# Attention output in a hybrid decoder layer: the probabilities become the weights, V with one column of ones is streamed, and the result is transposed by the crossbar

## The chip, the cores and the metric

The kernel runs on the 8 cores of one Trainium2 chip. Each core takes two of the sixteen sequences (4096 tokens) and all the weights, and exchanges nothing with the other cores. The time is device microseconds of the slowest core for one call. Matrix products run on TensorE (PE; PEld is its loading of weights), the rest on VectorE (DVE), ScalarE (ACT) and GpSimd (POOL); most transfers are issued from SyncE (SP).

## The reference, cut to what matters

One layer: a gated feed-forward half step, a mixing part, and a second gated feed-forward half step, all with RMS norms before them and residuals around them. The mixing part has causal latent attention (8 heads, 96 wide queries and keys, 64 wide values), a short gated convolution, sigmoid gates over both, and an output projection. The change touches only this:

```python
def one_block(args):
    qb, blk = args
    scores = jnp.einsum('bqhd,bkhd->bhqk', qb, k).astype(jnp.float32) * scale
    ...
    p = jax.nn.softmax(scores, axis=-1).astype(v.dtype)
    return jnp.einsum('bhqk,bkhd->bqhd', p, v)
...
y_a = causal_block_attention(q, k, v) @ w_proj_attn
```

x is (16, 2048, 1024) float32; D_FF is 2816. All products run in bf16 with float32 sums.

## The kernel before

**Order of the work.** Nobody writes the order of the instructions by hand. The program records operations with `op(eng, fns, cost, reads, writes)` and DMAs with `dma(...)`, each with a cost in microseconds, a key (how early it is wanted) and the tiles that it reads and writes. `Sched.order` then plays the program through four times with these costs, five queues (PE, ACT, DVE, POOL, SP), the PSUM banks and one DMA pipe, turns the place of each PE operation into due times for what feeds it (`deadlines`), and keeps the order with the shortest played length. `emit` writes each queue in that order with the semaphore waits that are needed. A queue runs strictly in its order: an instruction that waits holds up all behind it, on SP too. So an edit to one operation's cost or tiles can move instructions of every engine.

**Stages.** FFN1 over four blocks of 1024 tokens (L1061 gate and up, L1088 down), the mixing part over eight groups of 512 tokens (four per sequence), FFN2. In the mixing part the functions `qkv`, `attn`, `conv`, `merge` and `outp` of a group are recorded one after the other, and the scheduler interleaves groups: matmuls of the convolution and the merge fill PE while ACT makes the probabilities.

**Attention** (`attn`, L1260). For group g the query block is qb = g mod 4, and its key tiles are kt = 0 to 4 qb + 3, so 4, 8, 12 or 16 tiles of 128 keys. For each of 8 heads and each key tile:

- PE multiplies the 128 keys (weights) with the queries streamed, which gives scores with keys on partitions and up to 512 queries in the free dimension (L1273). On the four diagonal tiles only 512, 384, 256 and 128 queries are left.
- ACT takes the exponential into one of four bf16 tiles `pt` (L1277). On a diagonal tile POOL multiplies the first 128 columns by a triangle (L1280).
- PE multiplies `Vc` (weights) with `pt` streamed (L1282) and sums over the key tiles in one PSUM bank O. `Vc` holds, for each pair of heads, 64 columns of V, 64 of ones, and 64 of V of the other head. A 128 column window of it gives 64 partitions of output and 64 partitions that all hold the sum of the probabilities.

After a head's last key tile DVE makes four instructions (L1288, L1289, L1291, L1293): a transpose of the sums in 32 by 32 blocks from PSUM, a reciprocal of 16 columns, a transpose back, and the product of O with it, written to `atT` in bf16. `atT` has the attention output with channels on partitions, which is what the projection `ya` in `merge` streams (L1306, the rows `pb<-atT,rng`).

There are 640 (group, head, key tile) steps on a core: 448 with 512 queries, of which 384 are off the diagonal, and 64 each with 384, 256 and 128. O may take one of the banks 0 to 5, the scores too.

**Weights of the mixing part** come through a ring of eight tiles `rng` in pieces of eight matmuls (256 KB in bf16, four matmuls for `ya`), loaded by SP (`wpiece`, `dmm`, L1296 to L1306). The projections out of the latents are transposed by DMA_TRANSPOSE from SP, SBUF to SBUF (`ltT`, `KT`, `QT`). The V part of it is copied from PSUM to `Vc` by ACT (L1230), and its ones are written once by POOL (L1141).

**Memory** is laid out by hand: tiles of FFN2 share addresses with tiles of the mixing part, and the scheduler turns each overlap into a dependence. `U` (L684) is the address at which the tiles of the second half begin.

## Time and profile before

| | |
|---|---|
| three timed runs | 3454.61, 3130.39, 3073.76 us; median 3130.39 |
| the profiled execution | 3071.06 us |
| its span on the slowest core (core 7) | 3069.5 us |
| spans of the eight cores | 3061.7 to 3069.5 us |
| mean granted TensorE clock of each core | 0.998 to 1.000 |
| mixing part, about | 953 to 2119 us of the span |

The rows below are of core 7. Times in them are microseconds from the start of the span; a matmul's duration includes the time until its last result is written, so durations of consecutive matmuls overlap, and the time that one takes of PE is read from the distance of the starts. A row with "x8" merges eight consecutive instructions, and its length runs from the first start to the last end. Of the three timed runs the profiled execution is next to the fastest.

### The profile page before, as it was taken

How to read it: one execution, taken by the hardware profiler on the slowest of the kernel's cores; microseconds unless marked ns; L12 is line 12 of the kernel's file. 1: busy time of each engine (PE TensorE's matmuls, PEld its weight loads, DVE VectorE, ACT ScalarE, POOL GpSimd, SP SyncE). 2: the span in 40 equal slices, each digit the busy share in tenths (PEclk: the TensorE clock that was granted, in tenths of full speed). 3: DMA queues.
4: the chain of work that ended last, by engine and by line, in shares of the span. 5: the costliest groups of instructions: out<-in, count | busy, mean ns of one | idle time of the engine just before them, and what ended most of it. 6: DMA issues, size and time to landing. Idle time of an engine off the chain costs nothing.

```text
span 3069.5 us, 44192 instructions; the slowest of 8 cores (3061.7 to 3069.5 us)
## 1 busy us (share of the span) xinstructions
PE 3038.8 (99%) x14464; PEld 1408.0 (46%) x14464; DVE 1096.8 (36%) x1605; ACT 1008.2 (33%) x1798; POOL 754.3 (25%) x1415
## 2 busy tenths in 40 slices
PE   7999999999999999999999999999999999999999
PEld 3444444444444444444444444444444444444444
DVE  4232132133245564544755646443311121111111
ACT  2122112112124556668536475772210110110110
POOL 2111011111054544443645535321110000000000
PEclk9999999999999999999999999999999999999999
DMA  8967757997645676655785858567784564232212
GB/s 179 164 160 175 185 182 153 168 220 171 126 100 137 156 184 153 161 150 117 193 201 153 198 139 193 139 161 201 153 145 123 125 184 131 76 100 100 76 56 89
DMA packets 347980, 458.55 MB, mean 149 GB/s; under 512 B 200688, under 2 KB 210160, under 8 KB 346352
## 3 DMA queue, kind: packets, MB, share of 16 engines
q1 hardware_dynamic: 309744, 311.74, 38.9%
q0 software_dynamic: 31680, 120.93, 21.6%
q10 hardware_dynamic: 6336, 23.07, 1.9%
q8 instruction: 123, 2.02, 0.3%
q14 instruction: 97, 0.79, 0.1%
HBM read 394.63 MB, written 107.81 MB: 164 GB/s over the span
## 4 chain that ended last, share of the span: by engine, by line
PE 96%; DMA 1%; DVE 1%; issue 1%; POOL 0%; SPq 0%; ACT 0%; DVEq 0%; POOLq 0%; ACTq 0%
PE pb L1061 39%; PE pb L1306 22%; PE pb L1088 20%; PE pb L1282 4%; PE pb L1273 4%; PE pb L1375 4%; PE pb L1168 2%; PE pb L1207 1%; PE pb L1211 1%; DMA rng<-w 1%; DMA xr<-x 0%; DMA xin<-x 0%; ACT pt L1277 0%; SPq L1371 0%; DVE zb L1330 0%
## 5 line engine op out<-in xcount | busy, mean ns | idle before, releaser
L1061 PE MATMUL pb<-hT,gu 128*128 128x512 bf16 x5632 | 1220.2, 380 | 1.6 <-DVE hT L1010 1.6
L1061 PEld LDWEIGHTS pb<-hT,gu 128*128 128x128 bf16 x5632 | 551.5, 98 | 667.3 <-issue 5.2
L1088 PE MATMUL pb<-wd,actT 128*128 128x512 bf16 x2816 | 609.9, 379 | 0.0
L1065 ACT ACTIVATE sg<-pb 128x512 f32<-128x512 f32 x352 | 210.1, 597 | 1211.6 <-PE pb L1061 1211.6
L1306 PE MATMUL pb<-hM,rng 128*128 128x512 bf16 x2560 | 583.3, 379 | 0.9 <-ACT pt L1277 0.8
L1067 DVE TENSOR_TENSOR actT<-sg,pb 128x512 bf16<-128x512 f32 x352 | 241.9, 687 | 929.2 <-PE pb L1061 927.8
L1277 ACT ACTIVATE pt<-pb,negM,rK 128x512 bf16<-128x512 f32 (+3 forms) x640 | 409.9, 714 | 76.1 <-PE pb L1273 73.6
L1088 PEld LDWEIGHTS pb<-wd,actT 128*128 128x128 bf16 x2816 | 275.5, 98 | 331.7
L1306 PEld LDWEIGHTS pb<-hM,rng 128*128 128x128 bf16 x2560 | 249.3, 98 | 293.1 <-issue 3.0
L1092 DVE SCALAR_TENSOR_TENSOR xr<-pb,xr 128x512 f32<-128x512 f32 x128 | 88.3, 691 | 369.5 <-PE pb L1088 365.0
L1048 POOL DMA_DIRECT2D gu<-w x88 | 47.2, 536 | 663.1 <-PE pb L1061 575.4
L1350 DVE SCALAR_TENSOR_TENSOR tg<-tg,pb 128x512 f32<-128x512 f32 x128 | 87.9, 687 | 300.7 <-PE pb L1306 208.5
L895 POOL DMA_DIRECT2D gu<-ws x88 | 49.0, 557 | 549.3 <-DMA w<-gu 279.2
L1282 PE MATMUL pb<-pt,Vc 128*128 128x512 bf16 (+3 forms) x640 | 175.4, 348 | 3.2 <-POOL pt L1280 2.0
L1273 PE MATMUL pb<-QT,KT 96*128 96x512 bf16 (+3 forms) x640 | 173.0, 348 | 2.2 <-DVE atT L1293 1.2
L1280 POOL TENSOR_TENSOR pt<-pt,trib 128x128 bf16<-128x128 bf16 x256 | 108.9, 434 | 243.6 <-ACT pt L1277 238.4
L1353 POOL TENSOR_TENSOR mg<-tg,tg 128x512 bf16<-128x512 f32 x64 | 81.0, 1265 | 217.0 <-DVE tg L1350 216.5
L1347 ACT ACTIVATE tg<-pb,hb 128x512 f32<-128x512 f32 x128 | 88.2, 689 | 127.6 <-PE pb L1306 118.7
L1306 PE MATMUL pb<-cvT,rng 128*128 128x512 bf16 x512 | 120.8, 379 | 1.0 <-DVE cvT L1333 0.6
L1375 PE MATMUL pb<-rng,mg 128*128 128x512 bf16 x512 | 118.7, 379 | 0.7 <-ACT pt L1277 0.4
L1330 DVE SCALAR_TENSOR_TENSOR zb<-ub,par_sb,zb 128x512 f32<-128x512 f32 x128 | 102.8, 803 | 24.9 <-ACT zb L1328 20.8
L918 ACT ACTIVATE ho<-xr 128x1024 bf16<-128x1024 f32 x32 | 33.8, 1058 | 212.5 <-DVE xr L1092 203.4
(113 smaller groups left out, 1959.0 us busy)
## 6 DMA issues: line engine op xcount, KB each, us to landing
rng<-w SPq DMA_DIRECT2D x448, 256.0 KB, 3.7
gu<-ws POOLq DMA_DIRECT2D x88, 512.0 KB, 7.8
gu<-w POOLq DMA_DIRECT2D x88, 512.0 KB, 4.5
xr<-x SPq DMA_DIRECT2D x67, 512.0 KB, 5.0
w<-gu ACTq DMA_DIRECT2D x44, 512.0 KB, 4.9
w<-ws POOLq DMA_DIRECT2D x32, 522.0 KB, 21.6
x<-xr SPq DMA_DIRECT2D x32, 512.0 KB, 4.5
xm<-x SPq DMA_DIRECT2D x64, 256.0 KB, 6.1
```

Source lines behind the costliest of these rows:

```text
L1061: op("pe", [lambda e, k=k, a=a, b=b, i=i, sl=sl: e.matmul(bank(b), lhsT=gu[i][:, a, k, :], rhs=hT[sl][:, k, :], start=(k == 0), stop=(k == ...
L1065: op("act", lambda e, q=q, bg=bg: e.activation(out=sg[q][:], in_=bank(bg), func=AF.Silu), c_act(512), bg.deps, [d_sg[q]])
L1067: m = op("dve", lambda e, q=q, bu=bu, c=c, j=j: e.tensor_tensor(out=actT[:, j, c, :], in0=sg[q][:], in1=bank(bu), op=ALU.mult), c_dve(512) ...
L1088: op("pe", [lambda e, k=k, b=b, hf=hf, j=j, u=u: e.matmul(bank(b), lhsT=actT[:, j, k, u * 128:(u + 1) * 128], rhs=wd[:, k, hf * 512:(hf + ...
L1092: op("dve", lambda e, i=i, b=b, hf=hf: e.scalar_tensor_tensor(out=xr[i][:, hf * 512:(hf + 1) * 512], in0=bank(b), scalar=0.5, in1=xr[i][:, ...
L1273: op("pe", lambda e, h=h, kt=kt, j0=j0, n=n, s_=s_: e.matmul(bank(s_)[:, 0:n].rearrange("p (a b) -> p a b", b=128), lhsT=KT[kt // 4][0:96, ...
L1277: op("act", lambda e, i=i, s_=s_, n=n, kt=kt, h=h: e.activation(out=pt[i][:, 0:n], in_=bank(s_)[:, 0:n], func=AF.Exp, scale=rK[g // GPS][: ...
L1280: op("pool", lambda e, i=i: e.tensor_tensor(out=pt[i][:, 0:128], in0=pt[i][:, 0:128], in1=trib[:], op=ALU.mult), c_pool(128), [d_pt[i][0], ...
L1282: op("pe", lambda e, i=i, h=h, kt=kt, c0=c0, n=n, lo=lo, O=O: e.matmul(O()[:, c0:512], lhsT=Vc[kt // 4][:, kt % 4, h // 2, :, :].rearrange ...
L1306: op("pe", [lambda e, k=k: e.matmul(bank(b), lhsT=wv[:, k, :], rhs=rhs(k), start=(k == 0), stop=(k == K - 1)) for k in range(K)], c_mm(*[5 ...
L1330: op("dve", lambda e, q=q, k_=k_, w0=w0: e.scalar_tensor_tensor(out=zb[q][:], in0=ub[q][:, k_:k_ + 512], scalar=par[:, w0 + k_:w0 + k_ + 1 ...
L1375: op("pe", [lambda e, k=k, tt=tt, b=b, W=W: e.matmul(bank(b), lhsT=mg[:, k, tt * 128:(tt + 1) * 128], rhs=W[k // 2][0][:, (k % 2) * 512:(k ...
```

## The change

Operands of the second product are exchanged. For each 128 queries of a `pt` tile one matmul has these 128 columns of `pt` as weights and `Vc` of one head streamed, now 64 columns of V and a single one: 65 columns. Its output has queries on partitions: 64 channels and the sum, at columns 65j to 65j+64 of the same PSUM bank. The four query tiles of a step off the diagonal are one operation of four matmuls. On a diagonal tile the first query tile, which POOL masks, is an operation of its own, behind that of the others, so that the others don't wait for POOL. Query tile j is no longer multiplied with key tiles beyond its diagonal, as before.

A head then needs two DVE instructions: the reciprocal of four columns and the product of 4 times 64 columns with it, into the new tile `aq` (queries on partitions, bf16, one buffer for all groups). After the eighth head SP issues four DMA_TRANSPOSE, each of 128 queries by 512 channels, from `aq` to `atT`. `Vc` shrinks from 6 KB to 4.0625 KB a partition and sequence quarter, and about it all addresses move (`U` from 103.625 to 99.75); `r16` goes and `rec` becomes small.

```diff
-    r16, mk = sb("r16", [128, 16], F32)
-    d_r16 = [mk("0"), mk("1")]
+    rec, mk = sb("rec", [128, 2, 4], F32)
+    d_rec = [mk(f"{i}", 16 * i, 16 * i + 16) for i in range(2)]
...
-    U = 103.625
+    U = 99.75
...
-        t, mk = sb(f"Vc{i}", [128, TPG, 4, 3, 64], BF16)
+        t, mk = sb(f"Vc{i}", [128, TPG, NH, 65], BF16)
...
-        d_at.append([[mk(f"{c}{h}", c * 1024, c * 1024 + 1024) for h in range(2)] for c in range(4)])
+        d_at.append([mk(f"_{tt}") for tt in range(TPG)])
...
+    aq, mk = sb("aq", [128, TPG, 512], BF16)
+    d_aq = [[mk(f"{tt}{h}", tt * 1024 + h * 128, tt * 1024 + h * 128 + 128) for h in range(NH)] for tt in range(TPG)]
...
-        op("pool", lambda e, q=q: e.memset(Vc[q][:, :, :, 1, :], 1.0), 1.3, writes=d_V[4 * q:4 * q + 4], key=LB + 220 if q == 0 else MB - 250)
+        op("pool", lambda e, q=q: e.memset(Vc[q][:, :, :, 64:65], 1.0), 1.3, writes=d_V[4 * q:4 * q + 4], key=LB + 220 if q == 0 else MB - 250)
...
-            op("act", lambda e, st=st, v_=v_, p=p: e.activation(out=Vc[st // 4][:, st % 4, :, 0:3:2, :], in_=bank(v_).rearrange("p (a b d) -> p a b d", a=4, b=2),
+            op("act", lambda e, st=st, v_=v_, p=p: e.activation(out=Vc[st // 4][:, st % 4, :, 0:64], in_=bank(v_).rearrange("p (h d) -> p h d", h=8),
...
-                op("pe", lambda e, i=i, h=h, kt=kt, c0=c0, n=n, lo=lo, O=O: e.matmul(
-                    O()[:, c0:512], lhsT=Vc[kt // 4][:, kt % 4, h // 2, :, :].rearrange("p a d -> p (a d)")[:, lo:lo + 128], rhs=pt[i][:, 0:n],
-                    start=(kt == 0), stop=(kt == nkt - 1), skip_group_check=True),
-                   c_mm(n), [d_V[kt], d_pt[i]], [dO])
-            dn, p_ = 64 - lo, slice(lo, lo + 64)
-            dr, d16 = d_rec[h % 2], d_r16[h % 2]
-            op("dve", lambda e, p_=p_, dn=dn, O=O: e.transpose(out=rec[p_, :], in_=O()[dn:dn + 64, :]), 0.71, [dO], [dr])
-            op("dve", lambda e, p_=p_: e.reciprocal(out=r16[p_, :], in_=rec[p_, :].rearrange("p (b i) -> p b i", i=32)[:, :, 0]),
-               0.26, [dr], [d16])
-            op("dve", lambda e, p_=p_: e.transpose(out=rec[p_, :].rearrange("p (b i) -> p b i", i=32),
-                                                   in_=r16[p_, :, None].broadcast_to([64, 16, 32])), 0.71, [d16], [dr])
-            op("dve", lambda e, p_=p_, h=h, O=O: e.tensor_tensor(out=atT[ql][p_, h // 2, :], in0=O()[p_, :], in1=rec[p_, :],
-                                                                 op=ALU.mult), c_dve(512), [dO, dr], [d_at[ql][h // 2][h % 2]])
+                tiles = [j for j in range(j0, 4) if kt < 4 * qb or j > j0]
+                for first_, js in ((True, tiles), (not tiles, [j0] if kt >= 4 * qb else [])):
+                    if not js:
+                        continue
+                    op("pe", [lambda e, i=i, h=h, kt=kt, j=j, j0=j0, O=O, st_=(kt == 0 and first_ and j == js[0]): e.matmul(
+                        O()[:, j, 0:65], lhsT=pt[i][:, (j - j0) * 128:(j - j0 + 1) * 128], rhs=Vc[kt // 4][:, kt % 4, h, :],
+                        start=st_, stop=(kt == 4 * qb + j), skip_group_check=True) for j in js],
+                       0.031 * len(js), [d_V[kt], d_pt[i][0] if js == [j0] and kt >= 4 * qb else d_pt[i] if kt < 4 * qb else d_pt[i][1]], [dO])
+            dr = d_rec[h % 2]
+            op("dve", lambda e, h=h, O=O: e.reciprocal(out=rec[:, h % 2, :], in_=O()[:, :, 64]), 0.2, [dO], [dr])
+            op("dve", lambda e, h=h, O=O: e.tensor_tensor(out=aq[:, :, h * 64:h * 64 + 64], in0=O()[:, :, 0:64],
+                                                          in1=rec[:, h % 2, :, None].broadcast_to([128, 4, 64]), op=ALU.mult),
+               c_dve(256), [dO, dr], [d_aq[tt][h] for tt in range(TPG)])
+        for tt in range(TPG):
+            sc.key = MB + g * 100 - 87
+            dma("sp", f"aT{ql}{tt}", lambda e, tt=tt: e.dma_start_transpose(
+                out=atT[ql][:, :, tt * 128:(tt + 1) * 128], in_=aq[:, tt, :]), 200000, tr=True, reads=d_aq[tt], writes=[d_at[ql][tt]])
```

**Where instructions move.** First PE at the end of the last group's attention. In the kernel before, L1273 is the score product, L1282 the product with `pt` streamed, L1306 a piece of the convolution or of the merge (the numbers behind a name are those of its buffer and tile):

```order
L1306 MATMUL pb3<-hM1_115,rng6_155 128x512 x8
L1282 MATMUL pb1<-pt2_139,Vc2_132 128x512
L1282 MATMUL pb1<-pt3_140,Vc2_132 128x512
L1273 MATMUL pb0<-QT1_126,KT3_133 128x256
L1273 MATMUL pb1<-QT1_126,KT3_133 128x128
L1306 MATMUL pb3<-hM1_115,rng7_156 128x512 x8
L1282 MATMUL pb1<-pt0_137,Vc3_134 128x512
L1282 MATMUL pb1<-pt1_138,Vc3_134 128x384
L1306 MATMUL pb2<-hM1_115,rng0_149 128x512 x8
L1282 MATMUL pb1<-pt2_139,Vc3_134 128x256
L1282 MATMUL pb1<-pt3_140,Vc3_134 128x128
```

The same stretch of PE in the changed kernel, where the score product is L1272, the changed product L1285 and a piece L1309:

```order
L1285 MATMUL pb1<-Vc2_131,pt3_139 128x65 x4
L1272 MATMUL pb2<-QT1_125,KT3_132 128x256
L1309 MATMUL pb3<-hM1_115,rng7_155 128x512 x8
L1285 MATMUL pb1<-Vc3_133,pt0_136 128x65 x4
L1285 MATMUL pb1<-Vc3_133,pt1_137 128x65 x2
L1272 MATMUL pb1<-QT1_125,KT3_132 128x128
L1309 MATMUL pb3<-hM1_115,rng0_148 128x512 x8
L1285 MATMUL pb1<-Vc3_133,pt1_137 128x65
L1285 MATMUL pb1<-Vc3_133,pt2_138 128x65 x2
L1309 MATMUL pb0<-hM1_115,rng1_149 128x512 x8
L1285 MATMUL pb1<-Vc3_133,pt3_139 128x65
```

Each streamed 512 column product became four of 65 columns, and on the diagonal the masked query tile comes last. Behind this point the kernel before has seventeen pieces of eight matmuls ahead of the first `ya` (the row with `atT`); in the changed kernel the stretch of PE from the last of the attention to `ya` is short enough to show the last part of it whole:

```order
L1309 MATMUL pb3<-hM1_115,rng6_154 128x512 x8
L1309 MATMUL pb0<-hM1_115,rng7_155 128x512 x8
L1309 MATMUL pb1<-hM1_115,rng0_148 128x512 x8
L1309 MATMUL pb2<-hM1_115,rng2_150 128x512 x8
L1309 MATMUL pb2<-cvT_156,rng1_149 128x512 x8
L1309 MATMUL pb0<-atT1_141,rng3_151 128x512 x4
```

Four more such pieces stand ahead of these, so nine are left between the last product with `pt` and the first `ya`. In the other groups more PE work stands between the two, in both kernels.

On SP the four transposes of the last group stand among the loads of the ring in the changed kernel:

```order
L905 DMA rng0_148<-w2 128x1024
L905 DMA rng1_149<-w2 128x1024
L1296 DMA_TRANSPOSE atT1_141<-aq_167 128x4x128
L905 DMA rng2_150<-w2 128x1024
L1296 DMA_TRANSPOSE atT1_141<-aq_167 128x4x128 x3
L905 DMA rng3_151<-w2 128x512
L905 DMA rng4_152<-w2 128x1024
```

The loads of `rng2` and all behind it now stand behind a transpose that waits for the eighth head's DVE instruction; before, nothing of the attention's output stood on SP.

## Rows read from the trace of the kernel before

**Rows 1.** The page's first lines: span, busy time of each engine.

```profile
span 3069.5 us, 44192 instructions; the slowest of 8 cores (3061.7 to 3069.5 us)
PE 3038.8 (99%) x14464; PEld 1408.0 (46%) x14464; DVE 1096.8 (36%) x1605; ACT 1008.2 (33%) x1798; POOL 754.3 (25%) x1415
```

**Rows 2.** The chain of work that ended last, shares of the span by line.

```profile
PE pb L1061 39%; PE pb L1306 22%; PE pb L1088 20%; PE pb L1282 4%; PE pb L1273 4%; PE pb L1375 4%; PE pb L1168 2%; PE pb L1207 1%; PE pb L1211 1%; DMA rng<-w 1%; DMA xr<-x 0%; DMA xin<-x 0%; ACT pt L1277 0%; SPq L1371 0%; DVE zb L1330 0%
```

**Rows 3.** Stretches of the mixing part, 952 to 1100 and 1900 to 2062 us.

```profile
core 7: us, PE busy (x) PEld busy (x) DVE busy (x) ACT busy (x) POOL busy (x), PEclk, DMA share, GB/s
952.00:1100.00 148.00, 142.96 (x712) 68.41 (x711) 90.28 (x141) 91.65 (x165) 83.80 (x157) 0.98 0.58 134
1900.00:2062.00 162.00, 162.00 (x781) 75.31 (x779) 73.68 (x109) 116.69 (x191) 58.27 (x104) 1.00 0.63 164
```

**Rows 4.** Groups by line and shape: busy us, mean ns of one, idle before.

```profile
L1282 PE MATMUL pb<-pt,Vc 128*128 128x512 bf16 x448 | 143.6, 380 | 2.2 <-POOL pt L1280 1.0 <-ACT pt L1277 0.7 <-DVE atT L1293 0.5
...
L1282 PEld LDWEIGHTS pb<-pt,Vc 128*128 128x128 bf16 x640 | 62.1, 98 | 73.2 <-issue 7.5
...
L1282 PE MATMUL pb<-pt,Vc 128*128 128x384 bf16 x64 | 21.2, 331 | 1.0 <-POOL pt L1280 0.9
...
L1282 PE MATMUL pb<-pt,Vc 128*128 128x256 bf16 x64 | 17.6, 275 | 0.0
...
L1282 PE MATMUL pb<-pt,Vc 128*128 128x128 bf16 x64 | 14.1, 220 | 0.0
```

**Rows 5.** Timeline of PE: start us, length us, merged instructions.

```profile
26.63 0.61 PE L1008 MATMUL pb<-idb,xn 128*128 128x128 bf16 x8 [1.51 <-DVE xn L1004]
...
959.91 1.46 PE L1168 MATMUL pb<-wl,hM 128*128 128x384 bf16 x8
...
2061.76 29.52 PE L1306 MATMUL pb<-hM,rng 128*128 128x512 bf16 x136
```

**Rows 6.** Timeline of the weight loads (PEld), same columns.

```profile
962.13 0.10 PEld L1282 LDWEIGHTS pb<-pt,Vc 128*128 128x128 bf16 x1 [0.99 <-issue]
962.16 0.26 PEld L1273 LDWEIGHTS pb<-QT,KT 96*128 96x128 bf16 x2
...
1440.67 0.10 PEld L1273 LDWEIGHTS pb<-QT,KT 96*128 96x128 bf16 x1 [0.43 <-issue]
1440.71 0.10 PEld L1282 LDWEIGHTS pb<-pt,Vc 128*128 128x128 bf16 x1
...
1441.35 0.10 PEld L1273 LDWEIGHTS pb<-QT,KT 96*128 96x128 bf16 x1 [0.54 <-issue]
1441.38 0.10 PEld L1282 LDWEIGHTS pb<-pt,Vc 128*128 128x128 bf16 x1
```

**Rows 7.** Groups of DVE by line and shape.

```profile
L1288 DVE STREAM_TRANSPOSE rec<-pb 64x512 f32<-64x512 f32 x64 | 45.7, 714 | 52.2 <-PE pb L1282 51.1
L1291 DVE STREAM_TRANSPOSE rec<-r 64x512 f32<-64x512 f32 x64 | 45.1, 705 | 5.5
L1293 DVE TENSOR_TENSOR atT<-pb,rec 64x512 bf16<-64x512 f32 x64 | 44.0, 688 | 5.1 <-DVE rec L1291 0.5
...
L1289 DVE RECIPROCAL r<-rec 64x16 f32<-64x16 f32 x64 | 15.8, 248 | 6.0 <-DVE rec L1288 0.5
...
L1176 DVE TENSOR_TENSOR krb<-pb,par_sb 128x32 f32<-128x32 f32 x32 | 5.9, 186 | 7.1 <-PE pb L1168 6.8
```

**Rows 8.** The transposes of `ltT`: ns min/median/max on SP; then us to landing.

```profile
L1174 SPq DMA_TRANSPOSE ltT<-latn x32: 1183/1186/2188, 863.4 to 1907.5; - x32
...
ltT<-latn SPq DMA_TRANSPOSE x32, 3.2
```

**Rows 9.** What PE waited for, and for how long: us, times, longest.

```profile
PE pb L1306 <- DMA rng<-w: 3.5, 2, 3.1
```

**Rows 10.** Timeline of PE after the last group's attention.

```profile
2061.59 0.33 PE L1282 MATMUL pb<-pt,Vc 128*128 128x256 bf16 x2
...
2092.84 1.03 PE L1306 MATMUL pb<-atT,rng 128*128 128x512 bf16 x4
```

More of the change, by code:

```diff
@@ L707, in build_program @@
     d_gain1 = mk()
-    FF.append(ffn_tiles(2, 0, (28, 44.5, U + 50), 36, U, 52.5, U + 58))
+    FF.append(ffn_tiles(2, 0, (28, 42.5, U + 44.25), 36, U, 50.5, U + 52.25))
     at(0)
@@ L745, in build_program @@
     for i in range(2):
-        at((22, U + 50)[i])
+        at((22, U + 44.25)[i])
         t, mk = sb(f"hM{i}", [128, 8, G], BF16)
@@ L759, in build_program @@
     d_rpb = mk()
-    rec, mk = sb("rec", [128, G], F32)
-    d_rec = [mk("0"), mk("1")]
     ltT, d_ltT = [], []
@@ L773, in build_program @@
         if i:
-            at(U + 42)
+            at(U + 36.25)
         t, mk = sb(f"QT{i}", [128, TPG, NH, 128], BF16)
@@ L779, in build_program @@
     for i in range(GPS):
-        at(52.5 if i == 0 else U + 8 * (i - 1))
+        at(50.5 if i == 0 else U + 8 * (i - 1))
         t, mk = sb(f"KT{i}", [128, TPG, NH, 128], BF16)
@@ L783, in build_program @@
         d_KT += [mk(f"{q}", q * 2048, q * 2048 + 2048) for q in range(TPG)]
-        at(60.5 if i == 0 else U + 24 + 6 * (i - 1))
-        t, mk = sb(f"Vc{i}", [128, TPG, 4, 3, 64], BF16)
+        at(58.5 if i == 0 else U + 24 + 4.0625 * (i - 1))
+        t, mk = sb(f"Vc{i}", [128, TPG, NH, 65], BF16)
         Vc.append(t)
-        d_V += [mk(f"{q}", q * 1536, q * 1536 + 1536) for q in range(TPG)]
-    at(66.5)
+        d_V += [mk(f"{q}", q * 1040, q * 1040 + 1040) for q in range(TPG)]
+    at(62.5625)
     rK, d_rK = [], []
@@ L809, in build_program @@
         if i:
-            at(U + 66)
+            at(U + 60.25)
         t, mk = sb(f"atT{i}", [128, 4, G], BF16)
         atT.append(t)
-        d_at.append([[mk(f"{c}{h}", c * 1024, c * 1024 + 1024) for h in range(2)] for c in range(4)])
-    at(75.5)
+        d_at.append([mk(f"_{tt}") for tt in range(TPG)])
+    at(71.5625)
     ub, d_ub, zb, d_zb = [], [], [], []
@@ L828, in build_program @@
     assert place["o"] <= R0 + U * 1024
-    at(U + 58)
+    at(U + 52.25)
     cvT, mk = sb("cvT", [128, 8, G], BF16)
     d_cv = [mk(f"{c}", c * 1024, c * 1024 + 1024) for c in range(8)]
-    at(U + 70)
+    at(U + 64.25)
     mg, mk = sb("mg", [128, 8, G], BF16)
@@ L1264, in attn @@
             sc.key = MB + g * 100 - 95 + h
-            lo = 0 if h % 2 == 0 else 64
             ob = sc.slot(OB)
-            O, dO = lambda ob=ob: bank(ob), ob.deps
+            O, dO = lambda ob=ob: bank(ob).rearrange("p (j d) -> p j d", j=4), ob.deps
             for kt in range(nkt):
```

## The prediction

> **What bounds the kernel now.** I read the page's busy times first: PE is busy 3038.8 of 3069.5 us, no other engine over 36% [rows 1]. Then the chain that ended last: nearly all of it is PE, and the product that is changed (L1282) has 4% of the span [rows 2]. A share over the whole span can hide a stage with another limit, so the third view is the table of stretches of the mixing part [rows 3]. At its end PE is busy 162 of 162 us, with ACT at 117 and DVE at 74. At its beginning it is not quite so: PE 143 of 148, and the granted clock is 0.98, which with the two levels of 2.4 and 1.2 GHz is some 6 us at the lower one. So the kernel is bound by PE, and the change is worth what it takes off or puts on PE's own column of work; everything else counts only if it makes PE wait. The idle time that the mixing part offers is small: 5 us in the first stretch.
>
> Because PE's durations overlap, a matmul's price is the distance between starts. From merged rows it is (length minus the duration of one) over (count minus one) [rows 5, 4]: 512 columns (29.52 - 0.38)/135 = 0.216 us; 384 columns (1.46 - 0.33)/7 = 0.161; 128 columns (0.61 - 0.22)/7 = 0.056, each with a load of other weights between. These lie on one line of 0.000416 us a column, which gives 0.109 for 256.
>
> **PE: what goes.** L1282 has 448 matmuls of 512 columns and 64 each of 384, 256 and 128 [rows 4]: 448 x 0.216 + 64 x (0.161 + 0.109 + 0.056) = 96.8 + 20.9 = 117.6 us. The 4% of the chain (some 123 us) agrees.
>
> **PE: what comes.** 384 steps off the diagonal with four matmuls each, and 64 each with 4, 3, 2 and 1: 1536 + 640 = 2176 matmuls of 65 columns, each with its own load of 128 columns of `pt`. Nothing in the trace has 65 columns. Two things can set the distance:
>
> - The columns. The line above at 65 is 0.056 - 63 x 0.000416 = 0.030 us. A matmul of 65 columns cannot be cheaper than this by the rows, so it is the lower end: 2176 x 0.030 = 65 us, 52 less than before.
> - The load. A load's duration is 98 ns [rows 4], but loads overlap as matmuls do. After a stop of PE two loads of different tiles follow each other at 0.03, 0.04 and 0.03 us, with the first one's matmul issued in between [rows 6]. So a load, the start of its matmul and the next load fit in 0.033 us (the mean of the three, which are rounded to 0.01).
> - The upper end is the row of 128 columns: eight pairs of load and matmul at 0.056 us [rows 5]. A pair with fewer columns and the same load should not cost more: 2176 x 0.056 = 122 us, 4 more than before.
>
> I take the load's distance, 0.033, because it is the later of the two limits and is measured on the loads of this very product: 2176 x 0.033 = 71.8 us. The change on PE is 71.8 - 117.6 = -46 us, with ends at -52 and +4.
>
> The row of 128 columns bears on a rule. The Trainium skill, page "TensorE: Matmul & The Clock Gate", section "Back-to-back issue gap", says that in a stream of load and matmul pairs 128 columns cost about 81 ns each and 512 about 131. The trace has 56 and 216 for these, so it does not bear the rule out; by it 2176 pairs would be 176 us, 59 more than before.
>
> **Other engines.** DVE loses 0.714 + 0.248 + 0.705 + 0.688 = 2.36 us a head and gains a reciprocal of 4 columns and a product of 256. Between the rows of 32 columns (186 ns) and 512 (688 ns) [rows 7] the product is 0.42, and the reciprocal is no more than the 0.25 of 16 columns, say 0.2: 0.62 us. For 64 heads DVE goes from 151 to 40 us. It is off the path; the value on PE lies between 0 and the 5 us of idle and the 3 us of lower clock of the first stretch, where DVE is busy 90 of 148 us [rows 3]. I take 0, since ACT (92) and POOL (84) feed the same chain there. The memset of ones shrinks and the copy of V keeps its 512 columns: both are off the path, and I cost them at nothing under PE's own work.
>
> SP gains 32 transposes of 128 by 512. The nearest row is `ltT` with 128 by 640: 1.19 us on SP and 3.2 us to landing [rows 8]. That is 38 us of SP spread over 1100 us. Their path after the last head of a group is one product on DVE and its wait (0.7), four issues (4.8), one landing (3.2): 8.7 us, where before it was 2.4. `ya` waits for it. The shortest cover is in the last group: before, 31 us lay between the two [rows 10]; now nine pieces of eight matmuls are left, 72 x 0.216 = 15.6 us, so 7 us remain. Behind the first transpose on SP stand ring loads; when it waits for head 8, they wait. The ring holds eight pieces, 8 x 8 x 0.216 = 13.8 us of PE, against some 5 us of issues and the wait before. And the first head of the next group may not write `aq` before all four have landed; DVE would wait, and behind it the convolution's products. Each is covered by the rows, but a miss of some 3 us in a group, as the single wait for `rng` of 3.1 us shows now [rows 9], is possible. I put 0 in the sum, and 3 x 8 = 25 us at the far end.
>
> With PE 46 us faster over the mixing part, the last stretch would have ACT at 117 of some 150 us, still not a bound.
>
> **Sum.** The profiled execution took 3071.1 us (span 3069.5 and 1.6 around it): 3071.1 - 46 = 3025 us. The median of the three timed runs is 3130, 59 us above the profiled one; I forecast against the latter, which agrees with the fastest run within 3 us. 3025 is 1.5% less. About 2% (61 us) is what a measurement of this kernel can tell from no change.
>
> **Rivals.**
>
> 1. *The pair costs what 128 columns cost.* If a load cannot start until the array has taken the whole of the weights before it in, the distance of 0.03 after a stop is a burst and not a rate. Loads stood 0.056 apart in the long row of eight, but there the 128 columns alone explain that. Then 0.056 x 2176 = 122 and the time is 3071 + 4 = 3075. Anything between, say 0.045, gives 3051.
> 2. *PE gets faster, but waits give it back.* Place: merge of each group, by `atT` or by ring loads behind a waiting transpose on SP. Price up to 25 us, time 3025 + 10 to 25, 3035 to 3050. For it: the four queues are in fixed order, and SP is now on the attention's path. Against it: the covers above, 15.6 us against 8.7 at the tightest.
> 3. *More than the columns.* DVE's relief and the masked tile taken last remove the 5 us idle and the lower clock at the start of the mixing part, and the pair runs at the columns' 0.030: 3071 - 52 - 8 - 3 (the wait for `rng`) = 3008, just past 2% less.
> 4. *Slower: load and matmul take turns when the matmul is shorter than the load.* In all rows that I have, the matmul (216 to 380 ns from start to end, 56 or more between starts) covers the load's 98 ns. At 65 columns the load could stand in the open with its full 98 ns [rows 4]: 2176 x 0.098 = 213 us, 96 more than before, time 3167. It decides from 0.082 us a pair on (179 us for all), where the kernel is 2% slower. Against it: the loads 0.03 apart. By the rule of the Trainium skill above the time would be 3130, nearly this case; it shares this rival's chance.
>
> **How the numbers follow.** The forecast with its neighbourhood of 3010 to 3045 has 0.68; rival 1 and what lies between 0.13; rival 2 0.08; rival 3 beyond 2% 0.07; rival 4 0.04. The time is that of the likeliest, 3025. The range reaches from 3003, between rival 3 and the lower end of the pair's price, to 3078, which takes in rivals 1 and 2. Faster by over 2% (under 3010): 0.08. Slower by over 2% (over 3132): 0.04. Within 2%: 0.88.
>
> **What would show it.** The changed product's matmuls should stand 0.033 us apart in rows of four (a merged row of x4 about 0.1 us plus the duration of one), with loads at the same distance; 0.056 or 0.098 would be rivals 1 and 4. PE should still be busy 98 to 99% with a busy time some 46 us lower, DVE's some 111 us lower. In the waits of PE there should be no group `atT` or `rng` over 5 us; if there is, rival 2 holds. [...] The prediction is wrong if the span moves by less than 25 us, or if it moves by 46 for a reason that is not the distance of these matmuls.

## The result, and the profile of the changed kernel

The changed kernel takes 3028.5 to 3034.5 us, against 3073.0 to 3077.6 us of the kernel before; here and below, runs in which one die ran markedly slower at a lower clock are left out on both sides. The ratio is 0.9854, with a 95% interval of 0.9837 to 0.9871: 1.5% faster, some 45 us. The profiled execution of the changed kernel is the slowest of its four, 3034.5 us, and 37 us under the profiled one of the kernel before. The forecast was 3025 us and 46 us of gain.

The page's first lines, which answer to [rows 1] and [rows 2]:

```profile
span 3032.9 us, 47191 instructions; the slowest of 8 cores (3017.7 to 3032.9 us)
## 1 busy us (share of the span) xinstructions
PE 2990.5 (99%) x16000; PEld 1416.4 (47%) x16000; DVE 982.2 (32%) x1477; ACT 1004.2 (33%) x1798; POOL 748.2 (25%) x1415
...
PE pb L1061 40%; PE pb L1309 21%; PE pb L1088 20%; PE pb L1272 4%; PE pb L1378 4%; PE pb L1168 2%; PE pb L1285 2%; DMA rng<-w 1%; PE pb L1207 1%; PE pb L1211 1%; ACT pt L1276 0%; DMA xin<-x 0%; SPq L1296 0%; DVE zb L1333 0%; DMA h<-hq 0%
```

The profiled core is core 4 here, where it was core 7 before. PE has 1536 matmuls more and is busy for 48 us less; the changed product went from 4% to 2% of the chain (L1282 before, L1285 now). DVE lost 115 us. What PE is bound by has not changed.

The groups by line and shape answer to [rows 4] and [rows 7]:

```profile
L1285 PEld LDWEIGHTS pb<-Vc,pt 128*128 128x128 bf16 x2176 | 115.7, 98 | 80.6 <-issue 5.0
L1285 PE MATMUL pb<-Vc,pt 128*128 128x65 bf16 x2176 | 133.9, 194 | 2.0 <-POOL pt L1279 1.0 <-ACT pt L1276 0.6
...
L1291 DVE TENSOR_TENSOR aq<-pb,rec 128x256 bf16<-128x256 f32 x64 | 27.1, 424 | 6.0 <-DVE rec L1290 0.9
L1290 DVE RECIPROCAL rec<-pb 128x4 f32<-128x4 f32 x64 | 11.5, 180 | 66.6 <-PE pb L1285 65.6 <-PE pb L1272 0.8
```

A load still takes 98 ns and a matmul of 65 columns 194 ns from its start to its last result. What they take of PE is again read from the starts. The timeline of PE in the dense part of the last group (start us, length us, merged instructions), and the loads of the same stretch:

```profile
1975.59 0.41 PE L1285 MATMUL pb<-Vc,pt 128*128 128x65 bf16 x8
1976.06 0.29 PE L1285 MATMUL pb<-Vc,pt 128*128 128x65 bf16 x4
1977.48 0.41 PE L1285 MATMUL pb<-Vc,pt 128*128 128x65 bf16 x8
1979.40 0.41 PE L1285 MATMUL pb<-Vc,pt 128*128 128x65 bf16 x8
```

```profile
1975.38 0.50 PEld L1285 LDWEIGHTS pb<-Vc,pt 128*128 128x128 bf16 x8
1975.84 0.38 PEld L1285 LDWEIGHTS pb<-Vc,pt 128*128 128x128 bf16 x4
```

Eight matmuls in 0.41 us are (0.41 - 0.194)/7 = 0.031 us apart, four in 0.29 are 0.032, and four in 0.28, as in rows further down, 0.029. The expectations below use 0.029 or 0.030 for the same distance. With 0.031 the product costs 2176 x 0.031 = 67.5 us, 50 less than the 117.6 before. The row of eight loads is longer only because the first was pulled 0.2 us ahead, into the 512 column matmul before.

So 50 us went off PE's column and 45 off the time. What is between them is net waiting. Idle time of PE in the mixing part of core 7, kernel before and then changed (columns as in [rows 3]):

```profile
952.00:2100.00 1148.00, 1139.68 (x5623) 543.27 (x5622) 631.24 (x965) 695.16 (x1251) 536.11 (x980) 1.00 0.67 164
```

```profile
952.00:2100.00 1148.00, 1131.94 (x7360) 571.21 (x7358) 525.71 (x852) 703.47 (x1266) 541.20 (x989) 1.00 0.73 175
```

PE idles 8.3 us before and 16.1 after (on core 5, 10.8 and 20.3). The cores differ, though all run the same instructions: on the six whose records are complete it is 8.3 to 10.8 us before and 13.7 to 24.3 after. A difference of a few us on one core is therefore no finding by itself. Core 4, the slowest, has the most of these six. This is what happens on it at about 1038 us, PE's timeline and then the stretch:

```profile
1038.24 3.45 PE L1309 MATMUL pb<-cvT,rng 128*128 128x512 bf16 x8 [2.78 <-DMA rng<-w]
```

```profile
1036.00:1042.00 6.00, 3.76 (x10) 1.44 (x11) 0.13 (x1) 0.24 (x1) 0.00 (x0) 0.72 1.14 226
```

PE waits 2.8 us for a ring load, and the eight matmuls behind it span 3.45 us, where eight of this shape span 1.89 us otherwise. The granted clock of the stretch is 0.72, so part of it is at the lower level of 1.2 GHz. The same comes again about a wait of 3.6 us that ends at 1572.4. The mean clock of core 4 is 0.998, which is some 6 us of 3033. Core 7 has the first wait too (2.45 us), but no fall of the clock behind it, and not the second; its mean clock is 1.000, after 0.998 before, and its span fell by 48.7 us.

In the middle of the mixing part the waits are of another kind. On core 4 a stretch of 31 us in the later part of the fourth group's attention has 3.8 us of idle time, with ACT busy for 26.7 of 31:

```profile
1390.00:1421.00 31.00, 27.24 (x237) 14.79 (x234) 8.57 (x17) 26.74 (x50) 9.81 (x23) 1.00 0.61 132
```

The timeline of PE in it:

```profile
1408.91 0.38 PE L1272 MATMUL pb<-QT,KT 96*128 96x512 bf16 x1
1409.13 0.28 PE L1285 MATMUL pb<-Vc,pt 128*128 128x65 bf16 x4
1409.58 0.38 PE L1272 MATMUL pb<-QT,KT 96*128 96x512 bf16 x1 [0.17 <-ACT pt L1276]
1409.80 0.28 PE L1285 MATMUL pb<-Vc,pt 128*128 128x65 bf16 x4
1410.25 0.38 PE L1272 MATMUL pb<-QT,KT 96*128 96x512 bf16 x1 [0.17 <-ACT pt L1276]
1410.47 0.28 PE L1285 MATMUL pb<-Vc,pt 128*128 128x65 bf16 x4
```

Score product and changed product follow each other with no other work between. A step is 0.67 us here, the pace of one exponential on ACT, of which PE needs 0.22 + 0.12. Before, PE needed 0.43 of it. The profile shows only 0.17 us of the 0.33 that are lost in a step as idle: the rest is hidden under the durations of the matmuls, which overlap. So the idle times in this document are lower bounds of the waits.

What PE waited for, on core 4, against the single row [rows 9]:

```profile
PE pb L1309 <- DMA rng<-w: 9.6, 4, 3.6
PE pb L1309 <- DVE cvT L1336: 2.2, 2, 1.6
...
PE pb L1272 <- ACT pt L1276: 1.5, 7, 0.3
```

The waits for ring loads are longest on this core. On the eight cores they are 1.0 to 9.6 us, three of them over the 5 us of the forecast's sign for rival 2 (9.6, 7.4 and 5.1 us on cores 4, 5 and 6); before, they were at most 3.9 us. The transposes, against [rows 8] (their issues by tile, with shortest, median and longest ns; then the row of DMA issues, with the median us to the landing), and the way to `ya` in the last group (PE's timeline on core 7), against [rows 10]:

```profile
L1296 SPq DMA_TRANSPOSE atT<-aq x32: 1188/1194/2292, 986.4 to 2050.9; - x32
```

```profile
atT<-aq SPq DMA_TRANSPOSE x32, 4.4
```

```profile
2033.18 0.19 PE L1285 MATMUL pb<-Vc,pt 128*128 128x65 bf16 x1
2033.21 13.98 PE L1309 MATMUL pb<-hM,rng 128*128 128x512 bf16 x64
2047.03 1.89 PE L1309 MATMUL pb<-cvT,rng 128*128 128x512 bf16 x8
2048.76 1.03 PE L1309 MATMUL pb<-atT,rng 128*128 128x512 bf16 x4
```

`ya` starts 15.6 us after the last product and waits for nothing on this core. On core 4 it waits 1.55 us, not for `atT` but for its ring load, which SP had issued at 2052.3 us, behind the last three transposes (2048.2 to 2052.2). This is rival 2's mechanism, at 1.55 us; in the kernel before a later piece of `ya` waited 3.1 us for its load on core 7, with no transpose of `aq` on SP.

### The profile page after: what moved, and what is told of

Its sections match the earlier page's. It is cut to its first block, busy times and chain, and to the rows that moved or that the text cites. A ratio compares the mean times of both kernels' runs of the same rounds, so it can differ in the third digit from the quotient of the medians.

```text
span 3032.9 us, 47191 instructions; the slowest of 8 cores (3017.7 to 3032.9 us)
## 1 busy us (share of the span) xinstructions
PE 2990.5 (99%) x16000; PEld 1416.4 (47%) x16000; DVE 982.2 (32%) x1477; ACT 1004.2 (33%) x1798; POOL 748.2 (25%) x1415
## 4 chain that ended last, share of the span: by engine, by line
PE 95%; DMA 2%; issue 1%; DVE 1%; ACT 1%; POOL 1%; SPq 1%; DVEq 0%; ACTq 0%; POOLq 0%
PE pb L1061 40%; PE pb L1309 21%; PE pb L1088 20%; PE pb L1272 4%; PE pb L1378 4%; PE pb L1168 2%; PE pb L1285 2%; DMA rng<-w 1%; PE pb L1207 1%; PE pb L1211 1%; ACT pt L1276 0%; DMA xin<-x 0%; SPq L1296 0%; DVE zb L1333 0%; DMA h<-hq 0%
## 5 line engine op out<-in xcount | busy, mean ns | idle before, releaser
L1309 PE MATMUL pb<-hM,rng 128*128 128x512 bf16 x2560 | 586.8, 380 | 4.8 <-DMA rng<-w 3.6
L1309 PEld LDWEIGHTS pb<-hM,rng 128*128 128x128 bf16 x2560 | 248.7, 98 | 292.1 <-issue 9.8
L1272 PE MATMUL pb<-QT,KT 96*128 96x512 bf16 (+3 forms) x640 | 173.2, 347 | 3.1 <-ACT pt L1276 1.5
L1285 PEld LDWEIGHTS pb<-Vc,pt 128*128 128x128 bf16 x2176 | 115.7, 98 | 80.6 <-issue 5.0
L1285 PE MATMUL pb<-Vc,pt 128*128 128x65 bf16 x2176 | 133.9, 194 | 2.0 <-POOL pt L1279 1.0
L1309 PE MATMUL pb<-cvT,rng 128*128 128x512 bf16 x512 | 122.2, 382 | 6.6 <-DMA rng<-w 4.4
```

The lines of the kernel that those rows point to most:

```text
L1272: op("pe", lambda e, h=h, kt=kt, j0=j0, n=n, s_=s_: e.matmul(bank(s_)[:, 0:n].rearrange("p (a b) -> p a b", b=128), lhsT=KT[kt // 4][0:96, ...
L1285: op("pe", [lambda e, i=i, h=h, kt=kt, j=j, j0=j0, O=O, st_=(kt == 0 and first_ and j == js[0]): e.matmul(O()[:, j, 0:65], lhsT=pt[i][:, ( ...
L1309: op("pe", [lambda e, k=k: e.matmul(bank(b), lhsT=wv[:, k, :], rhs=rhs(k), start=(k == 0), stop=(k == K - 1)) for k in range(K)], c_mm(*[5 ...
```

## The experiments

Each kernel ran beside the kernel before on the same chip; a ratio is to that, with its 95% interval. The changed kernel has 0.9854 (0.9837 to 0.9871), and in a second measurement beside e13 to e15 0.985 (0.9816 to 0.9884).

### What sets the price of a 65 column matmul

**e1_cols33.** Half the columns, same loads, same order. The output has 32 values of a head twice, from an operation on DVE of the same size as before.

```diff
-                        O()[:, j, 0:65], lhsT=pt[i][:, (j - j0) * 128:(j - j0 + 1) * 128], rhs=Vc[kt // 4][:, kt % 4, h, :],
+                        O()[:, j, 0:33], lhsT=pt[i][:, (j - j0) * 128:(j - j0 + 1) * 128], rhs=Vc[kt // 4][:, kt % 4, h, 32:65],
-            op("dve", lambda e, h=h, O=O: e.reciprocal(out=rec[:, h % 2, :], in_=O()[:, :, 64]), 0.2, [dO], [dr])
-            op("dve", lambda e, h=h, O=O: e.tensor_tensor(out=aq[:, :, h * 64:h * 64 + 64], in0=O()[:, :, 0:64],
-                                                          in1=rec[:, h % 2, :, None].broadcast_to([128, 4, 64]), op=ALU.mult),
+            op("dve", lambda e, h=h, O=O: e.reciprocal(out=rec[:, h % 2, :], in_=O()[:, :, 32]), 0.2, [dO], [dr])
+            op("dve", lambda e, h=h, O=O: e.tensor_tensor(out=aq[:, :, h * 64:h * 64 + 64].rearrange("p a (b d) -> p a b d", b=2),
+                                                          in0=O()[:, :, None, 0:32].broadcast_to([128, 4, 2, 32]),
+                                                          in1=rec[:, h % 2, :, None, None].broadcast_to([128, 4, 2, 32]), op=ALU.mult),
```

> The product with pt as weights streams 33 columns (the upper half of V and the ones) instead of 65, with the same loads in the same order; it leaves out half of the output's channels (DVE writes the other half twice). In the changed kernel the pairs of load and matmul stand 0.029 us apart in the trace, not 0.033. Theory L, the load sets that distance and the columns are hidden under it: still 0.029, and a time within 4 us of the changed kernel's fast runs (3028.6). Theory C, the columns set it (65 columns are 0.029 by the line through the longer ones): with 33 the distance falls to the load's own limit, below 0.025, and the time by 2176 x 0.004 to 0.013 = 9 to 28 us, to 3000 to 3020.

Measured: 3017.1 and 3019.0 us, ratio 0.9825 (0.9804 to 0.9846). The groups and the timeline of PE:

```profile
L1285 PE MATMUL pb<-Vc,pt 128*128 128x33 bf16 x2176 | 119.1, 178 | 2.3 <-POOL pt L1279 1.4 <-ACT pt L1276 0.3
```

```profile
1968.57 0.36 PE L1285 MATMUL pb<-Vc,pt 128*128 128x33 bf16 x8
1971.90 0.36 PE L1285 MATMUL pb<-Vc,pt 128*128 128x33 bf16 x8
```

The distance is (0.36 - 0.178)/7 = 0.026 us: it fell from 0.031, so theory L is out, and columns set the price at 65. By the columns alone 33 would be 0.017, so at 33 something else binds, at 0.025 to 0.026, a little over the threshold that the expectation named. The time fell by 11 us, 2176 x 0.005.

**e2_cols128.** The same product with 128 columns.

```diff
-                        O()[:, j, 0:65], lhsT=pt[i][:, (j - j0) * 128:(j - j0 + 1) * 128], rhs=Vc[kt // 4][:, kt % 4, h, :],
+                        O()[:, j, 0:128], lhsT=pt[i][:, (j - j0) * 128:(j - j0 + 1) * 128],
+                        rhs=Vc[kt // 4][:, kt % 4, :, :].rearrange("p h d -> p (h d)")[:, min(h, 6) * 65:min(h, 6) * 65 + 128],
```

The matmul streams 128 columns of V that begin with the head's own 65; for the eighth head they begin one head earlier, so its output is that of the seventh. There is room for them: the code cuts the bank into four parts of 128 columns, and query tile j has columns 128j to 128j+64 in the changed kernel, not 65j to 65j+64 as the section on the change says.

> The same product streams 128 columns (V, ones and 63 columns of the next head, whose sums nobody reads), in the same order. Both theories of the pair: 0.056 apart, so 2176 x (0.056 - 0.029) = 59 us more of PE's column, 3088 if nothing else changes. Theory W, the changed kernel has lost some 10 us because PE now outruns ACT, POOL and DVE where attention is dense: a slower PE gets part of this back, 3075 to 3083. Theory X, the loss is from the four transposes and the ring loads behind them: the distance to them grows too, also below 3088, but the waits for rng shrink and those of the score products for ACT don't.

Measured: 3077.0 to 3086.8 us, ratio 1.0024 (1.0012 to 1.0036).

```profile
L1285 PE MATMUL pb<-Vc,pt 128*128 128x128 bf16 x2176 | 189.5, 219 | 1.5 <-POOL pt L1279 0.4 <-ACT pt L1276 0.3
```

```profile
1997.77 0.61 PE L1285 MATMUL pb<-Vc,pt 128*128 128x128 bf16 x8
2006.06 0.61 PE L1285 MATMUL pb<-Vc,pt 128*128 128x128 bf16 x8
```

The distance is (0.61 - 0.219)/7 = 0.056, as in the transposes of [rows 5]. The time rose by about 51 us (median 3080), where 2176 x (0.056 - 0.031) = 54 are added: a few of the waits went. This is also what the exchange of operands would have been worth without the short stream: nothing, or slightly slower. It is the upper end of the forecast's price and its rival 1 (3075), made real. The gain lies in the 65 columns.

### What gave back some of it

**e3_few_crossbar.** The transposes of six groups are left out.

```diff
-        for tt in range(TPG):
+        for tt in range(TPG if g < 2 else 0):
             sc.key = MB + g * 100 - 87
```

> The four transposes of aq are issued for groups 0 and 1 alone (8 of 32); later groups project the old atT, so the attention output of six groups is left out of the result. Theory X (transposes on SP and the ring loads behind them give back part of the gain): 4 to 10 us less than the changed kernel, 3019 to 3025, and waits of PE for rng back to 2 to 4 us. Theory W (PE outruns the engines that feed it): within 2 us of 3028.6.

Measured: 3028.5 to 3029.7 us, ratio 0.9861 (0.9843 to 0.9879), and on the slowest core

```profile
PE pb L1309 <- DMA rng<-w: 4.7, 4, 2.1
```

The time is the same, so theory X, 4 to 10 us, is out. Two limits: without the transposes the scheduler made another order, which by the runs further down can be worth more than such a difference, and the ring waits did not go (1.7 to 6.3 us on the eight cores, 1.0 to 9.6 in the changed kernel, 0.4 to 6.2 when it ran again as e12). So the ring waits are there with 8 transposes as with 32.

**e10_act_light.** ACT has 74 us less, the order is untouched (the traces have the same sequence on PE, ACT, POOL and DVE). From the third group on the exponential of an unmasked tile computes 256 of its 512 columns; the others keep old values.

```diff
-                op("act", lambda e, i=i, s_=s_, n=n, kt=kt, h=h: e.activation(out=pt[i][:, 0:n], in_=bank(s_)[:, 0:n], func=AF.Exp, scale=rK[g // GPS][:, kt, h:h + 1], bias=negM[:]),
+                op("act", lambda e, i=i, s_=s_, n=n, kt=kt, h=h, m=256 if g > 1 and kt < 4 * qb else n: e.activation(out=pt[i][:, 0:m], in_=bank(s_)[:, 0:m], func=AF.Exp, scale=rK[g // GPS][:, kt, h:h + 1], bias=negM[:]),
```

> Same instructions in the same order on every engine; off the diagonal, in groups 2 to 7, the exponential is made for 256 queries instead of 512 (the other half of pt keeps what an earlier step wrote, so the attention output of these queries is not that of the reference). ACT loses 352 x 0.21 = 74 us, all where attention is dense. Theory W (what the changed kernel gives back is PE waiting for the probabilities, and through them for pt tiles and banks): 4 to 10 us less than the changed kernel's 3028.6, with the row of small waits about 1392 to 1421 us gone. Theory D (it is transfers and the clock): within 2 us.

Measured: 3030.1 to 3033.6 us (one run 3042), ratio 0.9845 (0.982 to 0.9869). This chip ran the kernel before at 3081 or more, so the ratio is what can be compared: 0.1% below the changed kernel, some 3 us and within the intervals. In the mixing part of core 7:

```profile
952.00:2100.00 1148.00, 1136.22 (x7382) 573.06 (x7381) 526.15 (x852) 629.70 (x1268) 541.41 (x989) 1.00 0.71 175
```

PE idles 11.8 us instead of 16.1 on this core. But the changed kernel, run again as e12, has 13.7 here, and the other cores of this run with complete records have 13.2 to 16.7, so ACT's pace is worth some 2 to 4 us and that is not clear of the spread. Theory W's small waits went as it said (the score product waited 1.0 us for ACT's `pt` between 1300 and 1440 us on core 7, now 0.3), the longer ones did not: from 1390 to 1421 us PE still idles 2.9 us. It fell short of its 4 to 10 us in the time.

**e6_dve_back.** The last DVE product of each head is recorded four times more.

```diff
+            for _ in range(4):
+                op("dve", lambda e, h=h, O=O: e.tensor_tensor(out=aq[:, :, h * 64:h * 64 + 64], in0=O()[:, :, 0:64],
+                                                              in1=rec[:, h % 2, :, None].broadcast_to([128, 4, 64]), op=ALU.mult),
+                   c_dve(256), [dO, dr], [d_aq[tt][h] for tt in range(TPG)])
```

> The DVE product of each head is made five times instead of once: 4 x 64 x 0.424 = 109 us more on DVE, which is what the change had taken off it. If DVE's relief is worth nothing on the path, as forecast: within 3 us of 3028.6. If it is part of the gain: 5 to 15 us more, 3034 to 3044, with waits of PE for DVE in the mixing part.

Measured: 3033.2 to 3040.3 us, ratio 0.9889 (0.9873 to 0.9905): 0.35%, some 10 us slower. Part of it is the granted clock: none of the 32 cores of these runs has 1.000, where 19 of 32 have it in the changed kernel's. The mean is 0.001 lower, some 3 us. Here the scheduler planned around the extra work, so the order is another too.

**e11_dve_back_same.** The same 109 us inside the one operation, so that no queue changes its order; from a head's last product to the free bank DVE now has 0.18 + 5 x 0.424 = 2.3 us, as in the kernel before (2.36).

```diff
+    spare, _ = sb("spare", [128, 4, 4, 64], BF16, place["o"] + 2048)
...
-            op("dve", lambda e, h=h, O=O: e.tensor_tensor(out=aq[:, :, h * 64:h * 64 + 64], in0=O()[:, :, 0:64],
-                                                          in1=rec[:, h % 2, :, None].broadcast_to([128, 4, 64]), op=ALU.mult),
+            op("dve", [lambda e, h=h, O=O, x=x: e.tensor_tensor(out=aq[:, :, h * 64:h * 64 + 64] if x == 4 else spare[:, x, :, :],
+                                                                in0=O()[:, :, 0:64], in1=rec[:, h % 2, :, None].broadcast_to([128, 4, 64]),
+                                                                op=ALU.mult) for x in range(5)],
```

> The four extra DVE products of each head again, now inside the one recorded operation and into a spare tile, so that every queue keeps the changed kernel's order; 109 us more on DVE. The run before (3033 to 3040) let the scheduler plan for them. If DVE's relief itself is worth that much, 5 to 11 us more here too, or above, since nothing is planned around it; if the loss was the other order, within 3 us of 3028.6.

Measured: 3049.8 to 3053.3 us, ratio 0.9901 (0.9877 to 0.9925), on a chip where the kernel before took 3081 or more: 0.5%, some 15 us. On core 7 the mixing part, and what PE waits for:

```profile
952.00:2100.00 1148.00, 1114.31 (x7239) 560.61 (x7237) 600.32 (x1099) 696.70 (x1258) 535.87 (x983) 1.00 0.74 171
```

```profile
PE pb L1273 <- DVE aq L1292: 7.1, 10, 1.5
PE pb L1311 <- DMA rng<-w: 6.7, 2, 4.3
PE pb L1311 <- DVE cvT L1338: 3.8, 4, 1.6
```

PE idles 33.7 us, and 26.8 to 36.2 on the cores with complete records, all above the 13.7 to 24.3 of the changed kernel. DVE is at 600 of 1148 us and yet, with these products put back behind each head, PE's score product waits for the bank that DVE still reads (L1273 here is the score product). So DVE's relief is worth about 10 us where the scheduler may plan around the load and more where it may not; the forecast had priced it at 0.

### What the order is worth

**e8_price56.** The scheduler is told a price that is 1.8 times the measured one.

```diff
-                       0.031 * len(js), ...
+                       0.056 * len(js), ...
```

> Same operations, but the scheduler is told 0.056 us for one of the 65 column matmuls instead of 0.031, so it plans with a PE that is 54 us slower than the chip's. Theory O (order matters as much as the prices): it leaves less ACT and POOL work ahead of PE, PE catches up with it, and the time is 5 to 25 us above 3028.6. Rival: PE's backlog of convolution and merge covers any order, within 3 us.

Measured: 3016.8 to 3028.2 us on the chip where the kernel before took 3081 or more; ratio 0.9812 (0.9784 to 0.9839). The opposite of the expectation. In the mixing part of core 7:

```profile
952.00:2100.00 1148.00, 1141.41 (x7417) 575.97 (x7416) 526.32 (x857) 701.45 (x1277) 541.63 (x989) 1.00 0.73 177
```

PE idles 6.6 us instead of 16.1, less than the 8.3 of the kernel before; on the six cores with complete records it is 6.6 to 14.6 here, and 7.2 to 10.8 in e14_price56_mask. The plan made with the wrong price has denser attention: on core 7, 1300 us to the end of the fourth group's attention (1418 here, 1436 in the changed kernel), first this kernel, then the changed one:

```profile
1300.00:1418.00 118.00, 117.10 (x960) 62.33 (x959) 34.60 (x61) 103.62 (x176) 34.31 (x66) 1.00 0.54 135
```

```profile
1300.00:1436.00 136.00, 130.91 (x1010) 67.90 (x1009) 44.87 (x74) 108.78 (x181) 53.44 (x95) 1.00 0.58 142
```

ACT is busy 88% instead of 80%, with nearly the same work (104 and 109 us), and PE idles 0.9 us instead of 5.1.

**e4_mask_with_rest.** The masked tile is again in one operation with the others.

```diff
-                tiles = [j for j in range(j0, 4) if kt < 4 * qb or j > j0]
-                for first_, js in ((True, tiles), (not tiles, [j0] if kt >= 4 * qb else [])):
+                tiles = list(range(j0, 4))
+                for first_, js in ((True, tiles),):
```

> The masked query tile goes back into one operation with the others of its diagonal step, so the first matmul waits for POOL. POOL's instruction is 0.44 us and there are 256 such steps. If taking it last was worth something: 3 to 15 us above 3028.6 and waits for POOL L1279 above 3 us. If other work stands between anyway: within 3 us.

Measured: 3025.2 to 3032.2 us, same chip; ratio 0.9827 (0.9809 to 0.9846). Not slower; if anything faster by 0.2 to 0.3%, but the interval overlaps that of the changed kernel. PE's waits for POOL are 0.8 us in all, and it idles 10.2 us in the mixing part of core 7. So the split is not worth its place, or the other order that comes with the edit outweighs it. The two are not told apart by this run.

**e12_changed_again, e13_price45, e14_price56_mask** ran together. The edits of e13 and e14 are 0.045 for 0.031, and e8's together with e4's.

> The changed kernel once more, as the yardstick for the three that run beside it on this chip: 0.985 of the kernel before, 3028 us if that one is at 3073.

> The scheduler is told 0.045 us for a 65 column matmul (the chip takes 0.030). With 0.056 the kernel was 12 us faster than with 0.031, its waits of PE nearly gone. If that is a trend (a dearer product makes the plan keep convolution and merge matmuls for the dense part of attention): between the two, 0.981 to 0.985 of the kernel before. If each plan is a draw of its own: anywhere from 0.979 to 0.989, with no order in the price.

> Both edits that were each faster than the changed kernel: the price of 0.056 and the masked tile in one operation with the others. If their gains are of the same waits (some 22 us of PE's waiting in the changed kernel, 9 and 14 left in the two), little is left to win: 0.979 to 0.983 of the kernel before.

Measured: e12 3027.8 to 3030.1 us, ratio 0.985; e13 3023.3 to 3028.8, 0.9842 (0.9806 to 0.9877); e14 3013.8 to 3017.6, 0.9807 (0.9779 to 0.9835). e12 is as expected. e13 lies between e12 and e8, and its interval overlaps that of both, so it does not tell a trend from a draw. e14 is the fastest of the study, 13 us under the changed kernel beside it; its ratio is that of e8 within the intervals, so the two edits do not add up. Its mixing part on core 7:

```profile
952.00:2100.00 1148.00, 1140.18 (x7407) 574.50 (x7405) 528.75 (x856) 703.77 (x1272) 539.40 (x990) 1.00 0.74 176
```

7.8 us of idle time. Its matmuls and its work on ACT, DVE and POOL are those of the changed kernel, in another order.

**e15_before_dearer.** The kernel before, with its own product priced 1.45 times.

```diff
-                   c_mm(n), [d_V[kt], d_pt[i]], [dO])
+                   1.45 * c_mm(n), [d_V[kt], d_pt[i]], [dO])
```

> The kernel before with its own product with pt priced 1.45 times in the scheduler, which adds the same 53 us to the plan. If a dearer price helps because PE's column had become short against ACT (theory W), the kernel before, which waits 14 us in the mixing part, gains at most 2 us: 0.999 to 1.001. If it is a better way to plan for either kernel, 3 to 8 us: 0.997 to 0.999, and then the 12 us of the price are no part of what the change gave back.

Measured: 3064.0 to 3069.7 us, ratio 0.9972 (0.9955 to 0.9989), 8 to 9 us faster. So the dearer price gives a better plan for either kernel. Taken as they stand, the two ratios say that about two thirds of the 13 us that it wins in the changed kernel are not a repair of the change; their intervals are 5 and 8 us to either side, so this is a reading and not shown. Between the two kernels planned in this way the change is worth 0.9812/0.9972 = 0.984, an estimate of 49 us with some 10 to either side, against the 50 us that its matmuls take less. In the kernel before, the gain isn't in PE's idle time of the mixing part: it is 8.1 us on core 7, after 8.3. Part of it is in the granted clock: 62 of the 64 cores of its runs have 1.000, against 8 of 64 of the kernel before beside it, where most have 0.999; 0.001 is 3 us. In e14 it is 31 of 32, in e12 14 of 24. Why the other plan keeps the clock up, and what the rest of the gain is, stays open.

## Why the prediction was right, point by point

**The step on which the forecast rests held:** PE bounds the kernel, and the change is worth what it takes off PE's own column. PE's busy time fell by 48 us and the time by 45.

**The lower and the upper end of the pair's price** held: 0.031 lies between 0.030 and 0.056, and e2_cols128 gave the upper end its time (3080 against 3075).

**The value between them** was 0.033 and is 0.031, and its reason was wrong. The forecast took the load's distance for the later of two limits. e1_cols33 shows that load and matmul pairs go down to 0.026, so at 65 columns the columns are the limit. The three loads 0.03 to 0.04 apart [rows 6] follow a stop of PE and are no row of a running stream; that they show a start from rest is the likely reading, not a measured one. The term is 67.5 us instead of 71.8, and the saving 50 instead of 46.

**DVE's relief priced at 0** was wrong in size. DVE's own sum was right (0.18 + 0.42 us a head, 115 us less in all). But e6_dve_back and e11_dve_back_same show that the 109 us, put back, cost about 10 us with a plan for them (3 of them by the clock) and 15 without. This is their worth in the changed kernel, where PE is quicker; in the kernel before, DVE had this work and PE idled only 8.3 us. The chain of score product, exponential, product, DVE and bank is closed, so an engine that is half idle can still be late.

**Waits at 0** was wrong too, with the other sign. PE idles 8 to 10 us more in the mixing part on cores 7 and 5, and 24.3 us in all on core 4, where waits for ring loads and the clock that fell about them come on top. By the forecast's own sign (a group `rng` over 5 us) rival 2 would hold on three cores. Its size at the lower end (10 us) was right, its mechanism for the most part was not: with 24 of the 32 transposes gone time and ring waits stay as they are (e3_few_crossbar), and the one wait that stands behind transposes is 1.55 us. ACT's pace is some 2 to 4 us (e10_act_light), and most of the extra idle time goes with another order (e8_price56, e14_price56_mask). What in the order makes the ring loads late is not shown.

**The covers** held: 15.6 us of PE's work stood ahead of `ya` as worked out. The path took longer than the 8.7 us of the forecast, some 11 on core 7: DVE put one other instruction (0.75 us) between the head's two, SP a ring load between the transposes, and a landing took 4.4 us instead of 3.2. `ya` did not wait for `atT`.

**Rivals.** 1 (0.056) and 4 (0.098, load and matmul take turns) are out by the timeline: eight pairs in 0.41 us. The rule of the Trainium skill named with them ("TensorE: Matmul & The Clock Gate", "Back-to-back issue gap": about 81 ns for 128 columns in such a stream) is not borne out either: e2_cols128 has 2176 such pairs at 56 ns. The same section gives a floor of about 25 ns between starts however few the columns; e1_cols33 agrees with it at 26. Rival 3 was nearly right on the price (0.030) and right that DVE's relief counts, but wrong on the waits, which grew. The masked tile taken last brought nothing (e4_mask_with_rest). The granted clock did rise on core 7, from 0.98 to 1.00 in the first stretch, but it fell on cores 4, 5 and 6 (0.99 there), on core 4 about a wait for a ring load.

**Small slips.** The matmul durations of rival 4 are 220 to 380 ns (216 is a distance), and 3 x 8 is 24 us; neither moves a number of the forecast. That about 2% is needed to tell a change from none was too cautious: the interval is 0.17% to either side.

So the sum came out as -46 + 0 + 0 where the parts are -50 and +5: right within 2 us of the 45 measured. The mechanism is no luck, the closeness is: two terms, a saving and a wait, were each set too small and cancel. Between the two profiled executions, which the forecast took as its base, the gain is 37 us and the miss 9. The 5 us are what is left of the longer waits with DVE's relief already in them.

## What to carry to other kernels

Where the output of a product is narrower than what is streamed, exchange the operands: here 512 columns streamed became four times 65, each with 128 columns of weights loaded for it, and the price followed the columns down to at least 65, with a floor of 0.026 us that was met at 33. Price it by the distance of starts, not by the duration of load or matmul, and by rows from a running stream; rows just after a stop may show something else. Read a difference in idle time on all cores and in a second run of the same kernel before it is given a cause: here one kernel had 13.7 to 24.3 us. And when a list scheduler makes the order, a few per mille of difference can be the plan: measure the kernel before with the same freedom (other prices) before a change is credited or blamed for them.

## What the runs showed of the hardware that was not expected

A load of 128 columns of weights and a matmul of 33 columns fit in 0.026 us (e1_cols33), while each load is recorded with 96 ns: several loads and matmuls are under way at once. A DVE that is busy for 52% of the mixing part made PE wait 10 times for the bank that DVE still read, 7 us in all (e11_dve_back_same). In the changed kernel, where DVE is at 526 of 1148 us (46%), the same wait is in the list once, with 0.2 us: half of an engine's time free does not mean that it is never late. A wait of 2.8 us for one ring load is followed on core 4 by eight matmuls in 3.45 us instead of 1.89, with a granted clock of 0.72 in the 6 us about it: a late transfer costs its wait and can cost the clock behind it. It need not: core 7 waited 2.45 us at the same place and its clock stayed up.
